# Nine weight slots instead of six for the experts of a mixture-of-experts layer, in a one-core decoder step

## What is computed

```python
def expert_block(a):                       # one expert on its rows
    xb, e = a
    gate, up = jnp.split(xb @ w_gate_up[e], 2, axis=-1)      # 1024 -> 512 + 512
    return (jax.nn.silu(gate) * up) @ w_down[e]              # 512 -> 1024
```

## Time and profile before

| | us |
|---|---|
| runs | 2159.99, 2144.14, 2165.43 |
| profiled execution, its own time | 2152.84 |
| span of its profile | 2150.9 |
| experts of layer 0, first to last matmul | 651.3 to about 1212 |
| experts of layer 1, first to last matmul | 1585.8 to about 2116 |
| PE busy | 1699.6 (79%) |
| DMA, mean over the span | 281 GB/s |
| TensorE's granted clock, mean | 0.905 of full |

### The profile page before, as it was taken

One profiled execution on the slowest core, in us unless ns is written; L12 is line 12 of the kernel. 1 busy time (PEld: TensorE's weight loads), 2 busy tenths in 40 slices (PEclk: granted clock), 3 DMA queues, 4 the chain that ended last, 5 costly groups with the idle time before them and its releaser, 6 DMA issues.

```text
span 2150.9 us, 25298 instructions
## 1 busy us (share of the span) xinstructions
PE 1699.6 (79%) x8325; PEld 783.4 (36%) x8326; DVE 487.9 (23%) x1022; ACT 324.3 (15%) x601; POOL 121.9 (6%) x147
## 2 busy tenths in 40 slices
PE   5988687687947888787887679989748788788682
PEld 3433233345432433333332334434523333233231
DVE  1679344320150101000000132120410000000003
ACT  3022334222020000001110220000200011010001
POOL 0012000120120000000000100001010000000001
PEclk9999888798967999999999879999679999899996
DMA  9951586685047596999999930201468899999995
GB/s 353 416 172 70 204 306 235 228 301 227 0 161 311 214 414 259 401 419 417 423 423 420 350 139 0 79 0 41 195 243 329 324 416 422 421 423 422 421 423 214
DMA packets 144964, 604.27 MB, mean 281 GB/s; under 512 B 15952, under 2 KB 18289, under 8 KB 128362
## 3 DMA queue, kind: packets, MB, share of 16 engines
q1 hardware_dynamic: 113648, 522.55, 61.1%
q10 hardware_dynamic: 21025, 46.17, 5.7%
q0 software_dynamic: 10208, 34.48, 4.5%
HBM read 551.57 MB, written 52.01 MB: 281 GB/s over the span
## 4 chain that ended last, share of the span: by engine, by line
PE 63%; DMA 12%; DVE 10%; issue 7%; ACT 4%; POOL 1%; SPq 1%; ACTq 1%; DVEq 0%; POOLq 0%
PE ps L883 19%; PE ps L896 10%; PE ps L1008 8%; DMA ring<-in_w_gate_up_dram 5%; PE ps L578 5%; PE ps L594 3%; DMA ring<-in_w_down_dram 2%; PE ps L928 2%; PE ps L623 2%; PE ps L906 1%; DVE W L1483 1%; PE ps L940 1%; PE ps L520 1%; PE ps L496 1%; PE ps L718 1%
## 5 line engine op out<-in xcount | busy, mean ns | idle before, releaser
L883 PE MATMUL ps<-ring,W 128*64 128x512 f32 x2048 | 474.6, 615 | 48.3 <-issue 33.2
L896 PE MATMUL ps<-ring,W 128*64 128x512 f32 x1024 | 263.1, 659 | 54.7 <-DVE W L1806 49.3
L883 PEld LDWEIGHTS ps<-ring,W 128*64 128x64 f32 x2048 | 175.8, 141 | 335.1 <-issue 335.1
L1033 ACT ACTIVATE W<-ps 128x512 f32<-128x512 f32 (+3 forms) x244 | 138.1, 579 | 899.1 <-PE ps L896 353.8
L1800 DVE TENSOR_TENSOR W<-W,ps 128x256 f32<-128x256 f32 x64 | 27.0, 422 | 788.9 <-ACT W L1334 788.9
L1008 PE MATMUL ps<-hT,ring 128*128 128x512 f32 x384 | 168.0, 597 | 0.0
L896 PEld LDWEIGHTS ps<-ring,W 128*64 128x64 f32 x1024 | 88.0, 151 | 188.3 <-issue 188.2
L1008 PEld LDWEIGHTS ps<-hT,ring 128*128 128x128 f32 x384 | 72.8, 191 | 94.5 <-issue 94.5
L623 PE MATMUL ps<-ring,hT 128*128 128x512 f32 x192 | 88.6, 618 | 1.9 <-DVE W L1498 1.9
L1334 ACT ACTIVATE W<-ps 128x256 f32<-128x256 f32 x64 | 24.6, 384 | 423.3 <-PE ps L883 423.1
L1483 DVE SCALAR_TENSOR_TENSOR W<-W,prm 128x512 f32<-128x512 f32 x116 | 85.3, 805 | 0.0
(11 more groups left out here) (305 smaller groups left out, 1396.7 us busy)
## 6 DMA issues: line engine op xcount, KB each, us to landing
ring<-in_w_gate_up_dram SPq DMA_DIRECT2D x128, 2048.0 KB, 15.8
ring<-in_w_down_dram SPq DMA_DIRECT2D x64, 2048.0 KB, 15.0
ring<-in_w_ada_dram SPq DMA_DIRECT2D x24, 2048.0 KB, 9.1
x_rows<-X ACTq DMA_DIRECT2D x1, 18944.0 KB, 71.5
ring<-in_cache_k_dram SPq DMA_DIRECT2D x64, 256.0 KB, 3.2
W<-x_rows SPq DMA_DIRECT2D x32, 512.0 KB, 15.4
x_rows<-W ACTq DMA_DIRECT2D x128, 128.0 KB, 6.7
ring<-in_cache_v_dram POOLq DMA_DIRECT2D x48, 256.0 KB, 5.1
```

The source lines that it names most:

```text
L883: x = mm(ps[CAP * z:CAP * z + CAP, 2 + j, :], xt[:, k, :], at[:, :, 256 * z:256 * z + 256], start=(k == 0), stop=(k == KD - 1))
L896: x = mm(ps[CAP * z:CAP * z + CAP, 5 + j, :], ht[:, k % 2, CAP * (k // 2):CAP * (k // 2) + CAP], ring[:, 3 * j + 2, at:at + 512], start=(k ...
L1033: return fn(out, src, ACT.Copy, **k)
```

## The change

The slots become nine: six in `ring`, three laid over memory that is free while the experts run (`hT` and parts of the work area `W`, now one allocation `M_` with `Hb`). Expert n uses the slots of `j = n % 3` and the reload after expert n brings expert n+3. Before the experts start, the slots of expert 2 are filled too: two after the logits, one after the routing tables. The rows are fetched expert by expert (64 rows, 256 KB, into one half of the partitions) on ACT's queue, three experts ahead; they are turned expert by expert (8 transposes of 64 rows). `xT`, `hh`, `hhT` and the PSUM bank of the hidden transposes are single; `yh` is triple. The loop body is three experts, run ten times, and two follow. ACT gets a one-element silu ahead of the wait for gate and up. The sample gate, the repeated modulation rows and the routing's work area move to places outside the new slots; the spare rows in `x_rows` move up by 64.

```diff
 def slot(s):
+    return ring[:, s, :] if s < NSLOT else M_[:, M_SLOT[s - NSLOT]:M_SLOT[s - NSLOT] + SLOT]
 # SP
-                layer_wait(sp, l, "disp", 32 * NT)
-                rows_in(0, 0)
-                rows_in(1, 1)
-                step(0, 0, 2 * EG, pair=(2, 0))
...
+                layer_wait(sp, l, "h_ok", NT)
+                layer_wait(sp, l, "lg_mm", 1)
+                part(2 * EG, 2, 0)
+                part(2 * EG, 2, 1)
+                layer_wait(sp, l, "bounds", 1)
+                part(2 * EG, 2, 2)
+                def step(q, i):
+                    n, e = 12 * q + i, EG * ((i + 3) % G) + 3 * q + (i + 3) // G
+                    for k, name in enumerate(("g0_mm", "gu_mm", "down_mm")):
+                        sp.wait_ge(M[name], done(l, n))
+                        part(e, i % 3, k)
 # PE
-                def pair_turns(lane, count, p):
+                def x_turns(n, j, q):
+                    pe.wait_ge(x_in[j], q * 16 + (16 * FETCHES * l + 16))
...
-                        x = tr(ps[:, k // 4, P * (k % 4):P * (k % 4) + P], xg[:, lane, k:D:KD], ident)
+                        x = tr(ps[:, k // 4, CAP * (k % 4):CAP * (k % 4) + CAP], xg[j][:, k:D:KD],
...
-                    if nxt is not None:
-                        pair_turns(*nxt)
+                    if not last:
+                        x_turns(n + 1, (j + 1) % 3, q + (j + 1) // 3)
 # ACT
+                def rows_in(n, j):
+                    act.dma_start(xg[j], x_dram[bass.ds(CAP * n, CAP), :]).then_inc(x_in[j], 16)
...
+                layer_wait(act, l, "disp", 32 * NT)
+                for j in range(3):
+                    rows_in(j, j)
...
+                    if more:
+                        carry(act)
+                        rows_in(n + 3, j)
                     further(act, l, n, one_pass)
+                    fn(st[0:1, 91:92], st[0:1, 90:91], ACT.Silu)
                     act.wait_ge(M["gu_mm"], done(l, n))
-                    act.wait_ge(M["ht_mm"], done(l, n - 2))
+                    act.wait_ge(M["ht_mm"], done(l, n - 1))
...
-                    copy(flat(xT[:, lane, 0:4, :]), ps[:, 0, :]).then_inc(M["xa_ok"], 1)
+                    copy(flat(xT[:, 0:4, :]), ps[:, 0, 0:4 * CAP]).then_inc(M["xa_ok"], 1)
 # DVE
-                    v.tensor_copy(flat(xT[:, lane, 4:8, :]), ps[:, 1, :]).then_inc(M["xd_ok"], 1)
+                    v.tensor_copy(flat(xT[:, 4:8, :]), ps[:, 1, 0:4 * CAP]).then_inc(M["xd_ok"], 1)
 # all engines
-            with eng.Fori(0, E // 4 - 1) as q:
-                quad(q)
-            quad(E // 4 - 1, last=True)
+            with eng.Fori(0, E // 3) as q:
+                for j in range(3):
+                    step(3 * q + j, j, q, more=True)
+            for j in range(E % 3):
+                step(E - E % 3 + j, j, E // 3, last=j == E % 3 - 1)
```

More of the change, by code:

```diff
@@ L274, in ada_in @@
             return 16 if n < ADA0 else 16 * (n // 4 + 1 + (n % 4 > 0))
-        in1 = [in0[s] + 16 * PAIRS + (32 if s < 2 else 16) for s in range(NSLOT)]
+        in_layer = [16 * len(range(s // 3, E, 3)) for s in range(NRING)]
+        in1 = [in0[s] + in_layer[s] + (32 if s < 2 else 16 if s < NSLOT else 0) for s in range(NRING)]
         base_in = [in0, in1]
@@ L900, in pair_turns, with down @@
-                def pair_turns(lane, count, p):
-                    pe.wait_ge(x_in[lane], count * 16 + (16 * (PAIRS // 2) * l + 16))
-                    pe.wait_ge(M["xa_ok"], pdone(l, p - 1))
-                    pe.wait_ge(M["xd_ok"], pdone(l, p - 1))
+                    return x
+                def down(parts, j, strips):
+                    r, n = P // strips, D // strips
+                    for k, part in enumerate(parts):
+                        for z in range(strips):
+                            at = D * k + n * z
+                            x = mm(ps[r * z:r * z + r, 5 + j % 2, 0:n], part, slot(3 * j + 2)[:, at:at + n],
+                                   start=(k == 0), stop=(k == FE // P - 1))
+                    return x
@@ L936, in one_pass @@
-                        landed(j, 2, p)
-                        for k in range(4):
-                            for z in range(4):
-                                at = D * k + 256 * z
-                                x = mm(ps[XC * z:XC * z + XC, 5 + j, 0:256], hhT2[:, k, :],
-                                       ring[:, 3 * j + 2, at:at + 256], start=(k == 0), stop=(k == 3))
-                        x.then_inc(F["products"], 1)
-                    further(pe, l, n, one_pass, ways=(2, 2, 2, 2))
@@ L945, in step @@
-                    pe.wait_ge(M["xa_ok"], pdone(l, p))
-                    pe.wait_ge(M["xd_ok"], pdone(l, p))
-                    pe.wait_ge(M["h_ok"], done(l, n - 2))
-                    xt = xT[:, lane, :, CAP * j:CAP * j + CAP]
-                    landed(j, 0, p)
+                        pe.wait_ge(M["y_ok"], done(l, n - 1))
+                        landed(2)
+                        down([hhT2[:, k, :] for k in range(4)], j, 4).then_inc(F["products"], 1)
+                    further(pe, l, n, one_pass, ways=(2, 2, 2, 2))
@@ L961, in step @@
-                    landed(j, 2, p)
+                    for k in range(2):
+                        x = tr(ps[:, 7, P * k:P * k + P], hh[:, P * k:P * k + P], ident)
+                    x.then_inc(M["ht_mm"], 1)
+                    landed(2)
                     pe.wait_ge(M["ht_ok"], done(l, n))
-                    pe.wait_ge(M["y_ok"], done(l, n - 2))
+                    pe.wait_ge(M["y_ok"], done(l, n - 1))
                     carry(pe)
-                    down(hhT[:, j], j, M["down_mm"])
@@ L967, in ffn @@
-                pair_turns(0, 0, 0)
+                    down([hhT[:, k % 2, CAP * (k // 2):CAP * (k // 2) + CAP] for k in range(4)], j, 2).then_inc(
+                        M["down_mm"], 1)
+                x_turns(0, 0, 0)
                 each_expert(pe, step)
@@ L1039, in _ @@
                 act.sem_inc(M[n], AHEAD)
-            for j in range(2):
+            for j in range(3):
                 act.sem_inc(y_out[j], 32)
@@ L1360, in _ @@
             ffn(0, 6)
-            for j in range(2):
-                act.wait_ge(y_out[j], 32 * PAIRS + 32)
+            for j in range(3):
+                act.wait_ge(y_out[j], stored(1, j))
             h_rows(1)
@@ L1937, in ffn, with step @@
                 meet(pool, k0)
-                def step(n, j, p, lane, nxt=None):
+                def step(n, j, q, more=False, last=False):
                     def one_pass(c):
```

247 lines of the change are left out of this document (117 added, 130 removed).

## The result

The changed kernel takes 2186.74 us (median; 2180.3 to 2189.22), the kernel before 2154.84 beside it: a ratio of 1.0122, 95% interval [1.0066, 1.0179] (the quotient of the two medians is 1.0148, inside it). It is over 1% slower where 1.7% faster was forecast, and outside the range. The profiled execution took 2180.3 us, 2178.7 of it span.

A forecast was written before the change was run, and what follows sets the result against it. It took DMA to bound each layer's late part: 14.9 (third set) + 2.6 (table loads) + 0.5 (smaller copies) = 18.0 us a layer, 36 in all, from 2160.0 to 2124 us, range 2100 to 2150.

The forecast's parts named there:

- A transfer into 64 partitions: Row fetches beside the weight stream: half the partitions cost nothing, taken as 0, against 18 us a layer at half rate.
- rival C: Row fetches: half-width rows eat the gain; 2160 us at half rate for all engines, 2136 in a milder case; chance 0.19.
- the slot beside the dispatch: Third set's third load during the dispatch: fits in free DMA bandwidth, cost 0, bounds 0 and 5 us a layer.
- ACT's table load: Early silu ahead of the wait for gate and up hides table loads: 2.6 us a layer gained, bounds 0 and 9.0.
- loop bodies of three: Expert loop: three experts in a body cost 0.
- the third set's term: DMA-bound end of each layer: one expert's weights loaded before the stage starts, 14.9 us a layer gained.
- DMA decides: Late part of both layers: DMA, not PE, sets the gain, 2124 us, with bounds 2108 to 2138; chance 0.60.
- rival B: Expert stages: PE decides instead of DMA, 65 us gained, 2095 us; chance 0.10.
- Turning the rows of each expert: PE's transposes, hidden by the same expert's silu and product: cost 0, bounds -0.2 and +0.3 us per expert.
- The fetch on ACT's queue: Rows issued by ACT between its stores and silu: fits in ACT's order with 2.0 us to spare.
- rival D: ACT's queue between stores and the gate and up wait: silu comes 3.7 us late per expert, 2331 us; chance 0.07.
- E: Third set not loaded in time, or SP stands at its new waits: only table loads gain, 2154 us; chance 0.04.

The follow-up runs named there:

- e9: Kernel before, each pair's rows fetched as two DMAs of 64 rows into 64 partitions, issued by ACT one pair ahead: 2205.9 us, ratio 1.0265.
- e1: Kernel before, each pair's 128 rows fetched in two adjacent DMAs of 64 rows, one per half of the partitions, same queue: 2179.41 us, ratio 1.0125.
- e4: Changed kernel, an expert's 64 rows fetched as 128 half rows over all partitions, turned by sixteen products: 2140.93 us, ratio 0.996 to the kernel before.
- e2: Kernel before, each pair's full-width fetch of 128 rows issued by ACT one pair ahead: 2160.8 us, ratio 1.0033.
- e3: Changed kernel, each slot set reloaded one expert later, third set still filled before the stage: 2209.66 us, ratio 1.0266 to the kernel before.
- e7: Kernel before, each pair's rows fetched by two DMAs of 512 columns in all 128 partitions, same queue: 2159.29 us, ratio 1.0024.
- e5: Changed kernel, third part of the third slot set issued only after all dispatch tiles are scattered: 2186.27 us, ratio 1.0152 to the kernel before.
- e6: Changed kernel, ACT's early silu placed ahead of the extra passes instead of behind them: 2173.8 us, ratio 1.0082 to the kernel before.
- e12: Changed kernel with the edits of e4 and e6, third set's third part issued once the first expert's rows are turned: 2118.51 us, ratio 0.9872.
- e15: e12 measured once more, on the same chip as e14: 2119.61 us, ratio 0.9832 to the kernel before.
- e11: Changed kernel with the edits of e4 and e6, whole third slot set issued only behind the dispatch: 2134.1 us, ratio 0.9934 to the kernel before.
- e14: e13 with four 128 x 128 transposes per expert in place of eight products, halves sorted apart in the evictions: 2125.16 us, ratio 0.987.
- e8: Changed kernel with the edits of e4, e5 and e6 together: 2130.5 us, ratio 0.9876 to the kernel before.
- e10: Kernel before, each pair's rows as two 64-row DMAs on SP's queue with the down weights' DMA between them: 2208.72 us, ratio 1.0263.
- e13: e12 with x's chunks in another column order, eight 128-column products turning the rows, gate_up read in matching order: 2324.97 us, ratio 1.0773.

## Why the prediction was wrong

**The failed step is "A transfer into 64 partitions": "I take 0".** The bounds were 0 and 18 us a layer, and rival C, at half rate for all engines, gave 2160. The measured price is 0.9 to 1.1 us a fetch (changed kernel, e9) where half rate had 0.62; over the prediction's 29 fetches that is 26 to 32 us a layer, more than the 18 of gain. The rate at full share fell as the text had named for C: 391 and 399 GB/s for 418 and 422 in the same windows before. e1 shows it in the kernel before, e4 undoes it in the changed one, and e2, e3 and e7 take away queue, depth, number and size of the transfers as causes. The right case was there with 0.19, and even its upper end was too low. The reason for 0 was a poor one: the stores of 128 KB that leave 64 partitions and land in 5.9 us were in the kernel before all along, so whatever price they have is in its 422 GB/s already, and a landing time tells nothing of what other transfers lose. No run here changes the stores. The Trainium skill (SBUF — State Buffer, "Door 1: The DMA port swizzle") says that 64 partitions reach half the ports, and so half the rate. The runs agree with the direction, and e1 with the size (0.6 us). For a fetch alone beside a full stream they show more: 0.62 + 1.1 = 1.7 us for 256 KB, an estimate from the rates, which is some 36% of 422 GB/s.

**"I take 0" for the slot beside the dispatch** was wrong by 3 us a layer, inside its bounds of 0 to 5. Free bandwidth (2.3 MB of room for 2.1 MB) was the wrong measure: with the load in flight the last scatter takes 7.4 us and not 3.7. e5 adds that just behind the dispatch is no better a place, since there the load delays the first rows.

**"ACT's table load": the term of 2.6 us a layer** had its sign turned. The loads left the wait for gate and up, as said, but the early silu stands behind the extra passes, and the new loop body of three put passes ahead of a body's first silu: six new loads came up in them, with PE waiting. Moving the silu ahead of the passes removes them and gives 12 us by the medians, 6 to 8 by the profiled stages (e6). The text followed the load through the normal path only, and put loop bodies of three at 0. The 1.283 us a load hold. The 2.66 us a switch that the Trainium skill (ScalarE: Activation LUTs, "What ACT_TABLE_LOAD costs") gives are not seen in the periods, though the prediction's reading of them was a little off: in the kernel before an expert with turns takes 12.97 us and one without 12.77 (PE's gate products start at 1061.25 and 1074.02). The 14.16 us with a load belong to an expert without turns, so a load costs 1.39 and not 1.2.

**What held.** The size of the third set's term, 14.9 us a layer: with width and both small points mended, the kernel comes to 2119 us, 0.983 and 0.987 of before, where the forecast was 2124 of 2160, 0.983. The stages, first gate to last down product, are 16.3 and 20.4 us shorter than before in e12, 17.0 and 17.0 in e15, where the forecast had 18. But its reason, an expert's weights loaded "before the stage starts", is not what counts, as e11 shows: it is enough that the third set is full when the DMA-bound part begins. DMA decides at full width (e14 against rival B). Turning the rows of each expert costs nothing: the periods are 12.77 to 12.88 us where they were 12.77 and 12.97 in turn. The fetch on ACT's queue costs 0 at full width (e2). The silu starts 0.2 us behind PE's end, so rival D did not occur, nor did E: all nine slots are loaded before the first product (the last is issued at 637.33 and lands 10.4 us later). PE does not wait for the single inner buffers.

The three errors together: width 1.6% (e4 against the changed kernel), silu 0.7% (e6 against e5), the start 0 to 0.4% (e12 and e15 against e8), in sum 2.3 to 2.7%. From 1.012 to 0.987 and 0.983 it is 2.5 and 2.9%, so within the intervals nothing is left over.

## What to carry to other kernels

When a kernel is bound by a weight stream at share 1.0, don't cut another transfer to half the partitions: keep its bytes over all 128 (half rows as in e4, or two blocks in one DMA as in the kernel before), and if it must be narrow, put the complementary half right behind it in the stream's own queue (e1). Price a new transfer by what the stream loses, not by how fast it lands, and test it by putting that one line into the old kernel. A prefetch laid into "free" bandwidth delays whatever short transfer is on the critical path beside it; place it by what is waited for. Follow a hoisted table load into each conditional branch, and look again at where the loads fall when the number of experts in a loop body changes.

## What the runs showed of the hardware beyond that

- A fetch of 256 KB into 64 partitions beside a full stream takes 0.9 to 1.1 us of all engines more than into 128 (changed kernel, e9; e10 in layer 1, and 2.0 in layer 0); with its complement right behind it in the stream's queue, 0.6 (e1). Why it can be more than half rate's 0.62 stays open.
- With transfers in the queue that take some 40 us to land (43.66 and 41.28 us in the chain above), a single issue on SP's queue lasts up to 15.9 us in place of 0.33, and the rate doesn't suffer: 397 GB/s from 1100 to 1160 us, where issues are blocked, and 393 from 1000 to 1060, where nearly none is (changed kernel).
- Products of f32 over 128 x 128 with 64 columns took 3.95 us for eight chunks, and the granted clock behind them was 0.68 (e13). Sixteen products with a 128 x 64 operand took 2.1 us (e12) and four transposes of 128 x 128 0.75 (e14), both with 1.00 behind them. Eight were expected to be cheaper than sixteen; what sets them apart was not tested further.
